# A macaron decoder step in fp32 on one core: four PSUM banks for the down projections, and a new instruction order with weight splits on ScalarE and VectorE at both feed-forward entries

## The chip, the cores and the metric

One core of one Trainium2 chip runs the whole step. The metric is device time in microseconds of that core: 2587.69 us, the median of three runs (2587.02 to 2591.2). The engines are TensorE (PE in the profile, PEld for its weight loads), VectorE (DVE), ScalarE (ACT), GpSimd (POOL) and SyncE (SP), which here issues nearly all DMAs.

## The reference, cut to what matters

The model is one layer of a decoder trunk on 1024 prompt tokens and 8 sample tokens, 1032 in all, with width 1024 and hidden width 2816:

```python
def swiglu(x, w_gate, w_up, w_down):
    return (jax.nn.silu(x @ w_gate) * (x @ w_up)) @ w_down

def decoder_layer(x, pos, lp, attend):
    h = x + 0.5 * swiglu(rmsnorm(x, lp['norm_ffn1']), lp['ffn1_w_gate'], lp['ffn1_w_up'], lp['ffn1_w_down'])
    u = rmsnorm(h, lp['norm_mix'])
    ...
    h = h + merge_branches(o_mla.astype(h.dtype), o_dil.astype(h.dtype), gates,
                           lp['w_o_mla'], lp['w_o_dil'], lp['w_out'])
    h = h + 0.5 * swiglu(rmsnorm(h, lp['norm_ffn2']), lp['ffn2_w_gate'], lp['ffn2_w_up'], lp['ffn2_w_down'])
    return h, state
```

Everything is float32. The change touches the two `swiglu` lines only.

## The kernel before, in words

**Layout.** Activations are kept transposed: `x` is 128 partitions by 8 chunks (KD) of the width by 1032 tokens. The tokens form three tiles (TILES): 352, 352 and 328. The hidden width is 22 chunks of 128 (NF), taken as 11 pairs (NPAIR).

**Products.** Each float32 product is three passes of TensorE: both operands are split into an upper part, rounded to fp32r, and a lower part, the rest, and `mm3` (lines 803 to 805) multiplies hi by hi, lo by hi and hi by lo. The results gather in `ps`, eight PSUM banks of 512 floats.

**Weights.** They come as a stream of units of 128 x 1024 (512 KB). SP loads unit n into `raw` slot n % 2 once unit n - 2 is split (`split_done`). A split writes `w_hi` and then `w_lo` into slot n % 4. GpSimd does most of them (`split_unit`, lines 706 and 709, called by `split_units` and `split_straight`); ScalarE (`split_upper`, line 1459) and VectorE (`split_lower`, line 1858) do units 0 to 3 of the first feed-forward and two units of the projection. TensorE returns slots by `unit_used`. In the loops a feed-forward is a sequence of 66 units: two gates, two ups, and the downs of the pair before.

**Entry of a feed-forward.** The norm of the input isn't known when its first weights are there. So the first pair's gate and up run on the raw input (`first_gate_up`, line 837), in the order FIRST = (0,0), (1,0), (0,1), (0,2), (1,1), (1,2), each a chunk and a tile, each with a gate and an up group of 24 matmuls. `norm` (line 808 on, matmul at 818) sums the squares of a tile over the partitions. ScalarE takes the root (`root`, line 1474), VectorE the reciprocal (line 1854). VectorE then multiplies the gate by `rstd` (line 1923), ScalarE takes the silu (1531), VectorE the product (1931) and once more `rstd` (1934), ScalarE the upper part `h_hi` (1535), VectorE the lower `h_lo` (1937). Beside this the input itself is normalised for the later pairs, chunk by chunk: `xn` on VectorE (1877), `u_hi` on ScalarE (1482), `u_lo` on VectorE (416). From the second pair on `gate_up` (line 821) uses these, its first call waiting for each chunk in its gate groups (`normed`). All of this is written out by hand: every engine runs its own list in order, and semaphores tie them. The two lists are `first_hidden` of ScalarE (line 1524 on) and of VectorE (line 1912 on).

**Steady state.** For each later pair TensorE does two calls of `gate_up` (banks 0 to 2 gate, 3 to 5 up, one a tile), then `down` of the pair before: 24 blocks of six matmuls (8 output chunks by 3 tiles), which take turns in banks 6 and 7. There are ten such `down` in each feed-forward, 20 in all, and then `last_down`. VectorE adds each block to `x` (line 1959). The hidden part of the pair is made by `hidden` of both engines (ScalarE 1547 and 1551, VectorE 1950 and 1954). Block 0's addition stands between the last product of `hidden` and its last `h_lo` (the argument `between`). `down_evac` counts additions and starts at 2.

Of the kernel before, what the change touches and what calls it, by code (L numbers as in the profile page):

```python
# [29 lines left out]
P = 128  # L30
# [36 lines left out]
RING = 4  # L67
# [34 lines left out]
def build(nc, io):  # L102
    with ExitStack() as ctx:
# [320 lines left out]

        def ss_bank(q, t):
            return t if q == 3 else 6 + t % 2 if q != 1 else 4 + t
# [272 lines left out]
        def _(pool):  # L699
# [48 lines left out]
            split_units(RING, U_PROJ + 2)  # L748
# [43 lines left out]
            split_units(U_FFN2 + RING, N_UNIT)  # L792
# [5 lines left out]
        def _(pe):  # L798
# [38 lines left out]
            def first_gate_up(q, n, released):  # L837

                for i, (c, t) in enumerate(FIRST):
                    for j in range(2):  # L840
# [16 lines left out]
                        if j == 0 and i in (0, 2, 4):  # L857
                            norm(q, i // 2)

            def down_block(p, par, s, j, m, t):  # L860
                pe.wait_ge(down_evac, 24 * p + (j + 1))
                for c in range(2):
                    a, b = mm3(ps[:, 6 + j % 2, 0:TILES[t][1]], w_hi[:, s + c, m * P:(m + 1) * P],
# [6 lines left out]
            def down(p, par, n, s):  # L870

                pe.wait_ge(split_done, n + 2)
                pe.wait_ge(h_ready, 6 * p + 6)
                for m in range(KD):
                    for t in range(NT):
                        down_block(p, par, s, NT * m + t, m, t)

            def last_down(p, n, q):
# [3 lines left out]
                for t in range(NT):  # L882
                    for m in range(KD):
                        down_block(p, 0, 0, KD * t + m, m, t)
# [3 lines left out]
            def ffn(w, n0, released):  # L888
                f0, p0 = w * NF, w * NPAIR
                first_gate_up(2 * w, n0, released)  # L890
                for i in range((NPAIR - 1) // 2):
                    for half in range(2):
# [3 lines left out]
                        gate_up(4 * i + (f0 + 2 + 2 * half), 0, n, s, 2, normed=2 * w if i + half == 0 else None)  # L896
# [547 lines left out]
        def _(act):  # L1444
# [32 lines left out]
            def upper(q, t):  # L1477
                act.wait_ge(up_ready, 3 * NF * (q // 2) + FIRST.index((1, t)) + 1)
                for m in range(KD):
# [44 lines left out]
            def first_hidden(q):  # L1524

                for i, (c, t) in enumerate(FIRST):
                    w = TILES[t][1]
                    if c == 0 and t > 0:
                        root(q, t)
                    act.wait_ge(r_applied, R_BASE[q] + 2 * i + 1)  # L1530
                    A(silu[:, i % 2, 0:w], silu[:, i % 2, 0:w], ACT.Silu).then_inc(silu_done, 1)
                    act.wait_ge(h_mul, 3 * NF * (q // 2) + i + 1)
                    if i == 0 and q > 0:
                        act.wait_ge(down_ready, 24 * NPAIR - 23)
                    A(h_hi[:, 0, c, tile(t)], h32[:, i % 2, 0:w], ACT.Copy).then_inc(h_hi_done, 1)
                    if c == 1:
                        upper(q, t)
# [311 lines left out]
        def _(dve):  # L1849
# [62 lines left out]
            def first_hidden(q):  # L1912

                f0 = 3 * NF * (q // 2)
                for i, (c, t) in enumerate(FIRST):
                    w = TILES[t][1]
                    if c == 0:
                        reciprocal(q, t)
                        dve.wait_ge(r_done, 3 * q + t + 1)
# [5 lines left out]
                    if i == 0:  # L1925
                        raw_lower(q, 2)
                    dve.wait_ge(up_ready, f0 + i + 1)
                    dve.wait_ge(silu_done, f0 + i + 1)
                    if f0 + i > 1:
# [5 lines left out]
                                    ).then_inc(h_mul, 1)  # L1935
                    dve.wait_ge(h_hi_done, f0 + i + 1)
                    V.tensor_tensor(h_lo[:, 0, c, tile(t)], h32[:, i % 2, 0:w], h_hi[:, 0, c, tile(t)].bitcast(F32),
                                    ALU.subtract).then_inc(h_ready, 1)
                    if c == 1:
                        normed(q, t)  # L1940

            def hidden(f, c, par, between=None):
                for t in range(NT):
# [7 lines left out]
                    if t == NT - 1 and between is not None:  # L1951
                        between()
# [4 lines left out]
            def add_down_block(p, j, m, t):  # L1957
                dve.wait_ge(down_ready, 24 * p + (j + 2))
                V.scalar_tensor_tensor(x[:, m, tile(t)], ps[:, 6 + j % 2, 0:TILES[t][1]], 0.5, x[:, m, tile(t)],  # L1959
                                       ALU.mult, ALU.add).then_inc(down_evac, 1)  # L1960
# [672 lines left out]
```

## Time and profile before

| | |
|---|---|
| time, median of three runs | 2587.69 us (2587.02 to 2591.2) |
| span of the profiled execution, first to last instruction | 2584.7 us |
| TensorE busy | 2481.7 us, 96% |
| VectorE, ScalarE, GpSimd busy | 1113.6, 575.7, 881.2 us (43, 22, 34%) |
| mean granted clock of TensorE | 0.985 |
| matmuls | 16119, those of `u` and `h` in the feed-forwards and the projection by 0.32 us each |
| DMA | 229 MB, mean 89 GB/s; a weight unit lands 3.2 us behind its issue |

The profiled execution's own time isn't listed apart from the three runs, so it lies 2.3 to 6.5 us above its span, and the median 3.0 above it. Busy shares overlap: a matmul's row lasts 0.32 us, but the next one starts 0.16 us after it. A time is the start from the span's beginning. The first feed-forward runs from 12 to about 790 us, attention and merge from there to 1800, the second feed-forward to 2567, and the last norm closes the span. PEclk is the granted clock as a share of 2.4 GHz.

### The profile page before, as it was taken

How to read it: one execution, taken by the hardware profiler on the slowest of the kernel's cores; microseconds unless marked ns; L12 is line 12 of the kernel's file. 1: busy time of each engine (PE TensorE's matmuls, PEld its weight loads, DVE VectorE, ACT ScalarE, POOL GpSimd, SP SyncE). 2: the span in 40 equal slices, each digit the busy share in tenths (PEclk: the TensorE clock that was granted, in tenths of full speed). 3: DMA queues.
4: the chain of work that ended last, by engine and by line, in shares of the span. 5: the costliest groups of instructions: out<-in, count | busy, mean ns of one | idle time of the engine just before them, and what ended most of it. 6: DMA issues, size and time to landing. Idle time of an engine off the chain costs nothing. (4 is left out here: it accounts for less than half of the span.)

```text
span 2584.7 us, 40647 instructions
## 1 busy us (share of the span) xinstructions
PE 2481.7 (96%) x16119; PEld 2355.6 (91%) x16119; DVE 1113.6 (43%) x1936; ACT 575.7 (22%) x1328; POOL 881.2 (34%) x451
## 2 busy tenths in 40 slices
PE   6999999999999999999999888899999999999996
PEld 6899999999999998999765567899899999999996
DVE  7523232323236864311566456655833223222226
ACT  6300000000014441211555335113400000000002
POOL 2334443334445542433000111344244333344333
PEclk9999999999999999999999899899999999999998
DMA  5122212122223332421211354552111211111111
GB/s 183 56 72 89 78 65 89 69 95 72 78 82 129 135 113 100 149 94 73 73 45 43 97 210 160 176 173 73 66 68 69 91 41 49 49 50 49 41 41 66
DMA packets 85311, 229.45 MB, mean 89 GB/s; under 512 B 8889, under 2 KB 47330, under 8 KB 84034
## 3 DMA queue, kind: packets, MB, share of 16 engines
q1 hardware_dynamic: 79066, 207.90, 23.2%
q10 hardware_dynamic: 6088, 19.23, 1.9%
q8 instruction: 127, 2.08, 0.3%
q14 instruction: 30, 0.25, 0.0%
HBM read 196.69 MB, written 74.39 MB: 105 GB/s over the span
## 5 line engine op out<-in xcount | busy, mean ns | idle before, releaser
L803 PE MATMUL ps<-u_hi,w_hi 128*128 128x352 f32 (+1 forms) x2880 | 930.3, 323 | 30.5 <-DVE w_lo L1858 12.4
L804 PE MATMUL ps<-u_lo,w_hi 128*128 128x352 f32 (+1 forms) x2880 | 922.2, 320 | 0.0
L805 PE MATMUL ps<-u_hi,w_lo 128*128 128x352 f32 (+1 forms) x2880 | 920.4, 320 | 0.0
L706 POOL TENSOR_TENSOR w_hi<-raw,zero 128x1024 fp32r<-128x1024 f32 x178 | 340.2, 1911 | 1295.3 <-PE ps L803 1119.7
L803 PEld LDWEIGHTS ps<-u_hi,w_hi 128*128 128x128 f32 x2880 | 543.5, 189 | 39.2 <-DVE w_lo L1858 12.7
L804 PEld LDWEIGHTS ps<-u_lo,w_hi 128*128 128x128 f32 x2880 | 544.0, 189 | 0.9
L805 PEld LDWEIGHTS ps<-u_hi,w_lo 128*128 128x128 f32 x2880 | 543.0, 189 | 0.0
L709 POOL TENSOR_TENSOR w_lo<-raw,w_hi 128x1024 fp32r<-128x1024 f32 x178 | 437.1, 2456 | 13.9
L1959 DVE SCALAR_TENSOR_TENSOR x<-ps,x 128x352 f32<-128x352 f32 (+1 forms) x528 | 271.0, 515 | 211.9 <-PE ps L805 211.8
L1950 DVE TENSOR_TENSOR h<-ps,silu 128x352 f32<-128x352 f32 (+1 forms) x120 | 62.0, 516 | 679.4 <-PE ps L805 679.1
L803 PE MATMUL ps<-h_hi,w_hi 128*128 128x352 f32 (+1 forms) x1056 | 341.4, 323 | 4.7 <-DVE x L1959 2.2
L804 PE MATMUL ps<-h_lo,w_hi 128*128 128x352 f32 (+1 forms) x1056 | 338.0, 320 | 0.0
L805 PE MATMUL ps<-h_hi,w_lo 128*128 128x352 f32 (+1 forms) x1056 | 337.7, 320 | 0.0
L1547 ACT ACTIVATE silu<-ps 128x352 f32<-128x352 f32 (+1 forms) x120 | 55.0, 459 | 725.1 <-PE ps L805 725.1
L803 PEld LDWEIGHTS ps<-h_hi,w_hi 128*128 128x128 f32 x1056 | 198.4, 188 | 13.4 <-DVE x L1959 12.9
L804 PEld LDWEIGHTS ps<-h_lo,w_hi 128*128 128x128 f32 x1056 | 198.8, 188 | 0.2
L805 PEld LDWEIGHTS ps<-h_hi,w_lo 128*128 128x128 f32 x1056 | 198.7, 188 | 0.0
L1551 ACT ACTIVATE h_hi<-h 128x352 fp32r<-128x352 f32 (+1 forms) x120 | 59.1, 492 | 449.4 <-DVE h L1950 449.4
L1954 DVE TENSOR_TENSOR h_lo<-h,h_hi 128x352 fp32r<-128x352 f32 (+1 forms) x120 | 91.7, 764 | 58.1 <-ACT h_hi L1551 58.1
L2099 DVE TENSOR_TENSOR stage<-ps,rstd 128x352 f32<-128x352 f32 (+1 forms) x48 | 24.5, 515 | 142.1 <-PE ps L805 138.4
L1592 ACT ACTIVATE swapped<-ps 32x352 f32<-32x352 f32 (+1 forms) x144 | 64.7, 449 | 79.9 <-PE ps L805 61.6
L1072 PE MATMUL ps<-kT,qT 128*128 128x512 f32 (+3 forms) x192 | 74.3, 497 | 2.5 <-ACT probs L1700 2.4
(289 smaller groups left out, 2669.3 us busy)
## 6 DMA issues: line engine op xcount, KB each, us to landing
raw<-in_wstream SPq DMA_DIRECT2D x186, 512.0 KB, 3.2
out_win_out<-in_cache_win SPq DMA_DIRECT2D x23, 1424.0 KB
latn<-in_cache_mla SPq DMA_DIRECT2D x128, 80.0 KB, 1.8
scratch_gates<-stage ACTq DMA_DIRECT2D x16, 516.0 KB, 2.6
out_win_out<-in_cache_win SPq DMA_DIRECT2D x7, 1168.0 KB
kv_d<-in_cache_win SPq DMA_DIRECT2D x24, 256.0 KB, 7.4
sgt<-scratch_gates SPq DMA_DIRECT2D x16, 352.0 KB, 3.6
scratch_x_mid<-x SPq DMA_DIRECT2D x1, 4128.0 KB, 22.4
```

Of the source, the lines that this page charges most:

```text
L706: nc.gpsimd.tensor_tensor(hi, raw[:, s % RAW], zero[:].to_broadcast([P, UW]), ALU.add).then_inc(w_hi_done, 1)
L709: nc.gpsimd.tensor_tensor(lo, raw[:, s % RAW], hi.bitcast(F32), ALU.subtract).then_inc(split_done, 1)
L803: a = mm(out, wh, xh, start=start, stop=False)
L804: mm(out, wh, xl, start=False, stop=False)
L805: return a, mm(out, wl, xh, start=False, stop=stop)
L1072: last = mm(ps[:, bank, 0:w], qT[i % 2][h][:, n * P:(n + 1) * P], kT[i % 2][h][:, a * P:a * P + w], start=True, stop=not diag)
L1547: A(silu[:, b, 0:w], ps[:, t, 0:w], ACT.Silu).then_inc(silu_done, 1)
L1551: A(h_hi[:, par, c, tile(t)], h32[:, b, 0:w], ACT.Copy).then_inc(h_hi_done, 1)
L1592: last = A(swapped[a:a + 32, e % 2, 0:w], ps[b:b + 32, bank, 0:w], ACT.Copy)
L1950: V.tensor_tensor(h32[:, b, 0:w], ps[:, 3 + t, 0:w], silu[:, b, 0:w], ALU.mult).then_inc(h_mul, 1)
L1954: V.tensor_tensor(h_lo[:, par, c, tile(t)], h32[:, b, 0:w], h_hi[:, par, c, tile(t)].bitcast(F32), ALU.subtract).then_inc(h_ready, 1)
L1959: V.scalar_tensor_tensor(x[:, m, tile(t)], ps[:, 6 + j % 2, 0:TILES[t][1]], 0.5, x[:, m, tile(t)], ALU.mult, ALU.add).then_inc(down_evac, 1)
```

## The change

**Down projections.** The 24 blocks of `down` go round banks 0, 3, 6 and 7 in place of 6 and 7. A block waits for the addition four blocks back; the first two, in banks 0 and 3, wait for the silu and the product of tile 0 of the pair's second chunk, which read those banks. The next pair's first gate and up group wait for the additions of blocks 20 and 21. `between` is gone: VectorE adds block 0 with the others. `last_down` keeps banks 6 and 7.

**Entries.** Units 4 to 7 of each feed-forward's stream are split by ScalarE (upper) and VectorE (lower), so GpSimd begins with unit 8. The third sum of squares goes from behind the gate of (1,1) to behind that of (0,2). Both `first_hidden` are written anew, so that the work of (0,0) to (1,2) on the one side and the pieces of the normalised input and the splits on the other are interleaved.

```diff
+        DOWN_BANK = [0, 3, 6, 7]
...
-            split_units(RING, U_PROJ + 2)
+            split_units(2 * RING, U_PROJ + 2)
...
-            split_units(U_FFN2 + RING, N_UNIT)
+            split_units(U_FFN2 + 2 * RING, N_UNIT)
...
-            def gate_up(f, c, n, s, released, normed=None):
+            def gate_up(f, c, n, s, released, normed=None, after=None):
...
                         pe.wait_ge(silu_done if j == 0 else h_mul, 3 * f + (t - 2))
+                        if after is not None and t == 0:
+
+                            pe.wait_ge(down_evac, 24 * after + (23 + j))
...
-                        if j == 0 and i in (0, 2, 4):
-                            norm(q, i // 2)
+                        if j == 0 and i in (0, 2, 3):
+                            norm(q, (i + 1) // 2)
...
                 for m in range(KD):
                     for t in range(NT):
-                        down_block(p, par, s, NT * m + t, m, t)
+                        j = NT * m + t
+                        if j < 2:
+
+                            pe.wait_ge(silu_done if j == 0 else h_mul, 3 * (2 * p + 3) + 1)
+                        else:
+                            pe.wait_ge(down_evac, 24 * p + (j - 1))
+                        down_block(p, par, s, j, m, t, DOWN_BANK[j % 4])
```

ScalarE's new list, with `gated_silu(i)` for line 1531, `hidden_upper(i)` for 1535, `upper(q, t, part)` for the `u_hi` of some chunks:

```diff
+                unit = U_FFN2 * (q // 2)
...
+                for i in range(2):
+                    gated_silu(i)
+                    hidden_upper(i)
+                root(q, 1)
+                upper(q, 0, range(0, 2))
+                root(q, 2)
+                upper(q, 0, range(2, 3))
+                gated_silu(2)
+                upper(q, 0, range(3, 4))
+                hidden_upper(2)
+                split_upper(unit + RING)
+                upper(q, 0, range(4, 6))
+                split_upper(unit + RING + 1)
+                upper(q, 0, range(6, KD))
+                gated_silu(3)
+                hidden_upper(3)
+                gated_silu(4)
+                hidden_upper(4)
+                upper(q, 1)
+                gated_silu(5)
+                hidden_upper(5)
+                split_upper(unit + RING + 2)
+                split_upper(unit + RING + 3)
+                upper(q, 2)
```

VectorE's, with `scaled` for line 1923, `product` for 1931 and 1934, `hidden_lower` for 1937, and `next_normed(t, m)` for one `xn` and the `u_lo` of the chunk before:

```diff
+                reciprocal(q, 0)
+                scaled(0)
+                raw_lower(q, 2)
+                product(0)
+                scaled(1)
+                hidden_lower(0)
+                product(1)
+                normalize(q, 0, 0)
+                hidden_lower(1)
+                next_normed(0, 1)
+                reciprocal(q, 1)
+                scaled(2)
+                next_normed(0, 2)
+                product(2)
+                next_normed(0, 3)
+                hidden_lower(2)
+                split_lower(unit + RING)
+                next_normed(0, 4)
+                next_normed(0, 5)
+                split_lower(unit + RING + 1)
+                next_normed(0, 6)
+                reciprocal(q, 2)
+                next_normed(0, 7)
+                scaled(3)
+                lower(dve, V, q, 0, KD - 1)
+                product(3)
+                hidden_lower(3)
+                scaled(4)
+                normalize(q, 1, 0)
+                product(4)
+                next_normed(1, 1)
+                hidden_lower(4)
+                for m in range(2, KD):
+                    next_normed(1, m)
+                lower(dve, V, q, 1, KD - 1)
+                scaled(5)
+                product(5)
+                hidden_lower(5)
+                split_lower(unit + RING + 2)
+                split_lower(unit + RING + 3)
+                normed(q, 2)
...
             def add_down(p):
-                for j in range(1, NT * KD):
-                    add_down_block(p, j, j // NT, j % NT)
+                for j in range(NT * KD):
+                    add_down_block(p, j, j // NT, j % NT, DOWN_BANK[j % 4])
...
                         hidden(4 * i + (f0 + 2 + 2 * half), 0, 1 - half)
-                        hidden(4 * i + (f0 + 3 + 2 * half), 1, 1 - half, lambda: add_down_block(p, 0, 0, 0))
+                        hidden(4 * i + (f0 + 3 + 2 * half), 1, 1 - half)
                         add_down(p)
```

## Rows read from the trace of the kernel before

**Rows 1.** The waits of PE: engine, line, releaser: us in total, times, longest

```profile
PE ps L803 <- DVE u_lo L416: 6.8, 15, 2.8
...
PE ps L803 <- DVE x L1959: 2.2, 6, 1.2
```

**Rows 2.** Timeline, first down projection: start, us, engine, line, operation [idle before, releaser]

```profile
126.40 0.50 DVE L1950 TENSOR_TENSOR h<-ps,silu 128x328 f32<-128x328 f32 x1 [5.61 <-PE ps L805]
...
126.60 1.90 POOL L706 TENSOR_TENSOR w_hi<-raw,zero 128x1024 fp32r<-128x1024 f32 x1 [13.80 <-PE ps L803]
...
126.93 0.48 ACT L1551 ACTIVATE h_hi<-h 128x328 fp32r<-128x328 f32 x1 [3.70 <-DVE h L1950]
...
127.36 0.53 DVE L1959 SCALAR_TENSOR_TENSOR x<-ps,x 128x352 f32<-128x352 f32 x1 [0.47 <-PE ps L805]
...
127.80 1.05 DVE L1954 TENSOR_TENSOR h_lo<-h,h_hi 128x328 fp32r<-128x328 f32 x1
...
128.58 2.53 POOL L709 TENSOR_TENSOR w_lo<-raw,w_hi 128x1024 fp32r<-128x1024 f32 x1
...
128.78 0.95 DVE L1959 SCALAR_TENSOR_TENSOR x<-ps,x 128x352 f32<-128x352 f32 x2
128.88 0.31 PE L805 MATMUL ps<-h_hi,w_lo 128*128 128x328 f32 x1
...
129.34 0.43 PE L803 MATMUL ps<-h_hi,w_hi 128*128 128x352 f32 x1
```

**Rows 3.** Timeline, the same place of the twentieth down projection, TensorE

```profile
2518.01 0.43 PE L803 MATMUL ps<-h_hi,w_hi 128*128 128x352 f32 x1 [0.20 <-DVE x L1959]
```

**Rows 4.** Windows: us, PE, PEld, DVE, ACT, POOL busy (count), PEclk, DMA share, GB/s

```profile
54.15:68.43 14.28, 5.15 (x26) 4.99 (x26) 10.24 (x16) 9.38 (x13) 0.00 (x0) 0.76 0.33 121
63.40:66.20 2.80, 2.76 (x10) 2.76 (x11) 1.57 (x3) 1.59 (x2) 0.00 (x0) 0.50 0.00 0
79.73:89.40 9.67, 6.60 (x26) 4.99 (x25) 9.31 (x16) 4.03 (x9) 1.97 (x1) 0.82 0.18 57
91.77:99.35 7.58, 6.51 (x32) 4.50 (x30) 7.31 (x17) 4.11 (x9) 0.00 (x0) 1.00 0.00 0
93.26:99.97 6.71, 5.64 (x27) 3.71 (x26) 6.48 (x15) 3.27 (x8) 0.00 (x0) 1.00 0.00 0
1827.91:1831.52 3.61, 3.61 (x27) 3.61 (x26) 3.48 (x4) 3.13 (x5) 3.14 (x2) 1.00 0.02 5
1854.69:1862.64 7.95, 5.93 (x25) 4.85 (x25) 7.58 (x12) 2.69 (x6) 2.10 (x1) 0.79 0.42 143
1866.50:1873.20 6.70, 5.62 (x26) 3.71 (x26) 6.33 (x15) 3.25 (x8) 0.00 (x0) 1.00 0.00 1
```

**Rows 5.** Timeline of the first entry, engine by engine, merged where alike

```profile
38.08 0.53 DVE L1931 TENSOR_TENSOR h<-ps,silu 128x352 f32<-128x352 f32 x1 [1.01 <-ACT silu L1531]
...
44.65 2.56 POOL L709 TENSOR_TENSOR w_lo<-raw,w_hi 128x1024 fp32r<-128x1024 f32 x1
...
44.88 4.86 DVE L1877 SCALAR_TENSOR_TENSOR xn<-x,gains,rstd 128x352 f32<-128x352 f32 x2
...
58.06 1.28 ACT L1474 ACT_TABLE_LOAD   x1
59.36 0.55 ACT L1474 ACTIVATE rstd<-ps,eps 128x352 f32<-128x352 f32 x1
...
59.94 2.35 DVE L1854 RECIPROCAL rstd<-rstd 128x352 f32<-128x352 f32 x1 [1.34 <-ACT rstd L1474]
...
62.89 0.50 ACT L1531 ACTIVATE silu<-silu 128x352 f32<-128x352 f32 x1 [1.68 <-DVE silu L1923]
```

**Rows 6.** Timeline of the start: two splits of ScalarE and VectorE

```profile
9.74 1.99 ACT L1459 ACTIVATE w_hi<-raw 128x1024 fp32r<-128x1024 f32 x2
10.81 2.36 DVE L1858 TENSOR_TENSOR w_lo<-raw,w_hi 128x1024 fp32r<-128x1024 f32 x2 [0.31 <-ACT w_hi L1459]
```

More of the change, by code:

```diff
@@ L895, in ffn @@
                         n = 12 * i + (n0 + 4 + 6 * half)
-                        gate_up(4 * i + (f0 + 2 + 2 * half), 0, n, s, 2, normed=2 * w if i + half == 0 else None)
+                        gate_up(4 * i + (f0 + 2 + 2 * half), 0, n, s, 2, normed=2 * w if i + half == 0 else None,
+                                after=2 * i + (p0 + half - 1) if i + half > 0 else None)
                         gate_up(4 * i + (f0 + 3 + 2 * half), 1, n + 2, (s + 2) % 4, 2)
@@ L1475, in root, with upper @@
                   scale=1.0 / D).then_inc(std_done, 1)
-            def upper(q, t):
-                act.wait_ge(up_ready, 3 * NF * (q // 2) + FIRST.index((1, t)) + 1)
-                for m in range(KD):
+            def upper(q, t, part=range(KD)):
+                if part[0] == 0:
+                    act.wait_ge(up_ready, 3 * NF * (q // 2) + FIRST.index((1, t)) + 1)
+                for m in part:
                     e = KD * t + m
@@ L1524, in first_hidden, with gated_silu, hidden_upper @@
             def first_hidden(q):
[L1526 to L1529, printed above, removed]
+                unit = U_FFN2 * (q // 2)
+                def gated_silu(i):
+                    w = TILES[FIRST[i][1]][1]
                     act.wait_ge(r_applied, R_BASE[q] + 2 * i + 1)
                     A(silu[:, i % 2, 0:w], silu[:, i % 2, 0:w], ACT.Silu).then_inc(silu_done, 1)
+                def hidden_upper(i):
+                    c, t = FIRST[i]
                     act.wait_ge(h_mul, 3 * NF * (q // 2) + i + 1)
@@ L1534, in first_hidden @@
                         act.wait_ge(down_ready, 24 * NPAIR - 23)
-                    A(h_hi[:, 0, c, tile(t)], h32[:, i % 2, 0:w], ACT.Copy).then_inc(h_hi_done, 1)
-                    if c == 1:
-                        upper(q, t)
+                    A(h_hi[:, 0, c, tile(t)], h32[:, i % 2, 0:TILES[t][1]], ACT.Copy).then_inc(h_hi_done, 1)
+                for i in range(2):
[22 more added lines that the diff above has]
+                upper(q, 2)
             def hidden(f, c, par, p):
@@ L1914, in first_hidden, with scaled @@
                 f0 = 3 * NF * (q // 2)
-                for i, (c, t) in enumerate(FIRST):
+                unit = U_FFN2 * (q // 2)
+                def scaled(i):
+                    c, t = FIRST[i]
                     w = TILES[t][1]
-                    if c == 0:
-                        reciprocal(q, t)
-                        dve.wait_ge(r_done, 3 * q + t + 1)
+                    dve.wait_ge(r_done, 3 * q + t + 1)
                     dve.wait_ge(gate_ready, f0 + i + 1)
@@ L1924, in first_hidden, with product @@
                                     ).then_inc(r_applied, 1)
-                    if i == 0:
-                        raw_lower(q, 2)
+                def product(i):
+                    c, t = FIRST[i]
+                    w = TILES[t][1]
                     dve.wait_ge(up_ready, f0 + i + 1)
@@ L1935, in first_hidden, with hidden_lower, next_normed, hidden @@
                                     ).then_inc(h_mul, 1)
+                def hidden_lower(i):
+                    c, t = FIRST[i]
                     dve.wait_ge(h_hi_done, f0 + i + 1)
[L1937 to L1942, printed above, removed]
+                    V.tensor_tensor(h_lo[:, 0, c, tile(t)], h32[:, i % 2, 0:TILES[t][1]],
+                                    h_hi[:, 0, c, tile(t)].bitcast(F32), ALU.subtract).then_inc(h_ready, 1)
+                def next_normed(t, m):
+                    normalize(q, t, m)
+                    if m > 0:
+                        lower(dve, V, q, t, m - 1)
+                reciprocal(q, 0)
[39 more added lines that the diff above has]
+                normed(q, 2)
+            def hidden(f, c, par):
                 for t in range(NT):
```

19 lines of the change are left out of this document (9 added, 10 removed).

## The prediction, made before the changed kernel ran

> **What bounds the kernel now.** I began with TensorE's waits. Of the names of the feed-forwards two recur there: the pieces of `u_lo`, 6.8 us in 15 waits, and the additions into `x`, 2.2 us in 6 [rows 1]. These sums are too small, because a matmul's end is modelled and covers the first part of a stop, so I went on by start times. Every matmul of a feed-forward runs at 0.16 us start to start, so whatever TensorE stands still adds to the end, and what VectorE or ScalarE save elsewhere adds nothing.
>
> The first place is the down projection [rows 2]. Block 1 of a pair's 24 blocks is read out only after VectorE has made the last piece of `h_lo`: the product starts at 126.40, ScalarE's rounding at 126.93, block 0's addition is fitted in at 127.36, `h_lo` starts at 127.80 and is held until GpSimd's operation ends (1.05 us instead of some 0.52), and the additions of blocks 1 and 2 follow at 128.78. With two banks block 3 waits for block 1: TensorE's last matmul of block 2 starts at 128.88 and the next one at 129.34, 0.46 instead of 0.15, and that one takes 0.43 where 0.32 is usual. So a pair loses 0.31 + 0.11, some 0.41 us. The first of the 20 is shown; in the twentieth the stop is the same [rows 3].
>
> The second place is the entry of each feed-forward [rows 4]. A group of matmuls of the 352-wide tiles wants 3.86 us (24 by 0.161) and of the 328-wide 3.61, which the undisturbed group at 1827.91 shows. At the first entry the gate of (1,2), the last of FIRST, took 14.28, the normed gate of tile 1 9.67, that of tile 2 6.71: losses of 10.7, 5.8 and 3.1, in all 19.6 us. At the second entry the two normed gates took 7.95 and 6.70: 4.1 + 3.1 = 7.2 us. Behind them stand two causes. GpSimd splits units 4 to 7 here, and VectorE's operations on SBUF last as long as GpSimd's: two `xn` took 4.86 us beside a 2.56 us operation [rows 5], where eight `xn` with their eight `u_lo` took 7.58 with GpSimd idle, 0.95 a pair (the stretch 91.77:99.35) [rows 4]. And ScalarE's order puts the eight `u_hi` of tile 0, a Sqrt table load (58.06), a reciprocal (2.35) and the load of Silu ahead of the silu for which the gate waits, which comes at 62.89 [rows 5].
>
> **The change: down projections.** Four banks (0, 3, 6, 7) take turns, and block 0's addition no longer comes between. `h_lo` could start at 127.46 (0.53 after the rounding's start); it is still held until GpSimd ends at 128.5, so it ends at about 128.85, and blocks 0 and 1 are added from 128.78 and 129.25 [rows 2]. Block 4 is the first that waits for an addition, block 0's, done at 129.30. Its turn on TensorE comes at 129.99 (129.03 plus six matmuls). Slack 0.65. From there an addition takes 0.47 against 0.96 for a block, so VectorE catches up. What is queued behind the later additions is only other additions. The gate and up of the next pair now wait for blocks 20 and 21; block 20 is read out while 21 to 23 are computed. The first two blocks wait for silu and product of tile 0, some 15 us old. The added waits of TensorE (two a pair) I cost at nothing, since groups with two waits run at full rate; the bounds are 0 and 20 by 0.1. Sum: 20 by 0.41 = **8.1 us**, ends 6 and 8.3.
>
> The Trainium skill (TensorE: Matmul & The Clock Gate, "A second HAM failure mode: psum-queue depth-cycling") speaks against this part: cycling through PSUM banks made one kernel's clock swing. This trace, with two banks, can't show it for four; what it would do here is rival 3.
>
> **The first entry.** Up to the product of (0,0) at 38.08 the order is the old one [rows 5]. From there I walked the new order with the rows' own distances: 0.44 to 0.5 from one VectorE operation to the next, 0.56 where the second reads the first, 0.55 to 0.6 over to ScalarE and back, 2.35 and 2.20 for a reciprocal, 1.28 for a table load [rows 5], 1.0 for a split's upper half on ScalarE and 1.15 to 1.2 for its lower on VectorE [rows 6], all without GpSimd, which now splits nothing between weight units 3 and 8. It gives:
> - product of (1,0) at 40.3, `xn` 0 and 1 and `h_lo` by 42.9; Sqrt loaded to 43.2, root of tile 1, two `u_hi`, root of tile 2 by 45.1;
> - reciprocal of tile 1 44.6 to 47.0, scaling 47.0, third `xn` 47.5, its `u_hi` 48.1, Silu loaded 48.6 to 49.9, silu of (0,1) at 49.9, product 50.5 (was 63.5). The gate of (1,2) needs that silu at 54.15, so it no longer waits: 10.7 us gone, with the low clock in it.
> - `xn`/`u_lo` 3 to 5 with weight unit 4 (lower half 54.0) and unit 5 (58.2 to 59.4), then reciprocal 60.2 to 62.4, scaling of (0,2) at 63.4, silu 63.9 to 64.4. TensorE reaches the first normed gate at 61.4 (54.15 + 3.61 + 3.61) and waits for this silu: a new stall of 3.0 us.
> - tile 1: first `xn` 67.0, last `u_lo` done 77.0. TensorE, at 64.4 + some 1.3 for a low clock + 2 by 3.86, needs the first at 73.5: no stall.
> - silu, product of (1,2) and `h_lo` to 80.1, lower halves of units 6 and 7 80.6 to 82.9, then the eight pairs of tile 2, 7.58 us for eight as from 91.77 to 99.35 [rows 4], to 90.5. The gate ends 0.62 behind the last, at 91.1, against 99.97. TensorE, there at 81.4, stands or is paced for 6.1 us.
>
> Gain **8.9 us**. The bound at the end is VectorE's queue alone, so the 3.0 us stall and its clock cost nothing more. The low clock is in the rows: over 63.40:66.20, behind the long stop, it was 0.50 (1.2 GHz) and ten matmuls filled 2.8 us, 1.3 us more than ten at 0.16 do [rows 4]; in the new order that falls in time that tile 2's wait would take anyway.
>
> **The second entry.** The chain is the same, but the root of tile 2 waits for its sum of squares, a matmul moved behind the gate of (0,2), which ends just before 1828.2 [rows 4]; ScalarE and then VectorE stand 4 to 5 us. Root 1828.8, `u_hi` 1829.2, table to 1831.0, product of (0,1) 1831.6: 1781.1 behind the first entry. Here TensorE reaches the normed gate at 1847.1, 1.6 behind the silu, so that stall is absent. Tile 1's pieces end at 1858.1, which TensorE wants from 1854.9 to 1858.3: at most 0.2 lost. Tile 2's end at 1871.6 and the gate at 1872.3, against 1873.20. Gain **0.9 us**: 4.1 saved at tile 1, and nearly all given back at tile 2, since the two halves of four splits (4.7 us on VectorE) take the place of the waits for GpSimd.
>
> A table switch on ScalarE costs 1.28 us in the row, with the Sqrt 0.02 behind its end (58.06 and 59.36) [rows 5]. The Trainium skill (ScalarE: Activation LUTs, "What ACT_TABLE_LOAD costs") puts a drain of about 1.4 us behind each. By that rule two more such terms would stand in each chain and the sum would be smaller by 4 by 1.4 = 5.6 us; the trace disagrees, as the next activation follows at once.
>
> **What hides the rest.** Unit 6 loads once unit 4 is split (55 instead of 47) and is wanted at 79.5; unit 8 loads once unit 6 is (82) and GpSimd wants it at about 95. SP's queue has only these in it. Its window copy stands behind unit 7's load and slips to about 60; nobody waits for it. GpSimd's units 8 and 9 are released by the second gate as before and take 2 by 4.5 us (as at 126.60 and 128.58) [rows 2], with 4 by 3.86 + 2 by 3.61 = 22.7 us before the down needs them. Without that cover each would cost its whole lateness. What GpSimd is spared at each entry lies beside TensorE and brings nothing directly.
>
> **Sum.** 8.1 + 8.9 + 0.9 = 17.9 us off a span of 2584.7. The median of the three runs is 3.0 above the span and I keep that distance: 2587.7 - 17.9 = **2569.8 us**. Bounds: each entry's walk has some 50 handoffs that the old order doesn't show; at 0.05 either way, 2.5 us an entry, up or down.
>
> **Rivals.**
> 1. The entries bring much less. VectorE is the bound at both; if the wait for ScalarE between half splits is longer, or other operations are held, each microsecond counts fully. For: two of its queues have no slack. Against: GpSimd is idle in this stretch. With the whole gain of the entries lost but 2 us: 2577.6.
> 2. The bank ring brings nothing, the wait going from block 3 to block 4. That takes `h_lo` held 0.65 us longer in each pair. Against: the same operation ends at GpSimd's boundary whether it starts at 127.46 or 127.80. Entries alone: 2577.9. That the ring isn't what it says I exclude: all readers' and writers' waits change together.
> 3. The ring of banks lets TensorE's clock fall in the down projections. Place: each of 20 downs. Price: 1.3 us for a low stretch as at 63.40, so 20 by 1.3 = 26 against 17.9 gained: 2569.8 + 26 = 2595.8. It decides from 14 downs with such a stretch (18.2). Against: the clock is 1.00 in the rows where TensorE is paced for 6.7 us in small waits (from 93.26 and 1866.50) [rows 4], and the ring removes a wait.
>
> **Numbers.** A measurement of this kernel can tell about 0.2%, 5.2 us. Forecast 0.77, rival 1 0.11, rival 2 0.05, rival 3 0.03, other losses within 0.2% 0.04. The bounds of the forecast reach from 2565.5 (entries better by 2 each) to about 2575; the milder half of rival 1 takes the upper end to 2576.5, and 0.17 to 0.18 stays outside. Faster: 0.77 + 0.11 + 0.05 = 0.93; same 0.04; slower 0.03.
>
> **What would show it.** Right: no `x` entry in TensorE's waits, 24 down blocks of 0.91 to 0.97; the gate of (1,2) in 3.6 us; a stall of 3 us near 61 in the first entry and none in the second; the gates of tile 2 ending near 91.1 and 1859.3 (1872.3 less 8.9 and less ten downs by 0.41); VectorE's `xn` at about 0.57 each in both. Wrong: downs that stop at block 4, `xn` of 2 us and more, or a second entry that ends over 2 us from its place.

## The result, and the profile after

The changed kernel takes 2565.51 us (median of 4 runs, 2564.88 to 2567.56) against 2587.44 in the same comparison: faster by 21.9 us. The ratio of the timed runs is 0.9912, with a 95% interval of 0.9897 to 0.9926 (the plain quotient of the two medians is 0.9915). The forecast was 2569.8, a ratio of 0.9931, with a range that ended at 2565.5, 0.9914. Direction and mechanism held; the gain was 4 us larger than forecast, and the ratio lies just beyond the range's end, by less than its own uncertainty.

The page of the changed kernel, its span and its busy row:

```profile
span 2563.5 us, 40664 instructions
...
PE 2470.6 (96%) x16119; PEld 2355.6 (92%) x16119; DVE 1106.8 (43%) x1944; ACT 577.9 (23%) x1332; POOL 845.0 (33%) x435
```

The waits of its TensorE, where [rows 1] stood, with the one on the silu:

```profile
PE ps L805 <- DVE u_lo L416: 5.5, 3, 2.7
...
PE ps L805 <- ACT silu L1545: 2.9, 1, 2.9
...
PE ps L805 <- DVE x L2048: 1.7, 3, 1.2
```

The kernel before had this line for the silu:

```profile
PE ps L803 <- ACT silu L1531: 9.1, 1, 9.1
```

The waits for `u_lo` are 3 instead of 15, and no wait for `x` is from a pair's down any more: the three that remain belong to the last down at the end. The wait for the silu was one of 9.1 us and is another one of 2.9. The first down projection, in the timeline, answers to [rows 2]:

```profile
116.87 0.50 DVE L2041 TENSOR_TENSOR h<-ps,silu 128x328 f32<-128x328 f32 x1 [5.61 <-PE ps L807]
...
117.08 1.90 POOL L708 TENSOR_TENSOR w_hi<-raw,zero 128x1024 fp32r<-128x1024 f32 x1 [13.80 <-PE ps L805]
...
117.40 0.48 ACT L1591 ACTIVATE h_hi<-h 128x328 fp32r<-128x328 f32 x1 [3.69 <-DVE h L2041]
...
117.92 1.41 DVE L2043 TENSOR_TENSOR h_lo<-h,h_hi 128x328 fp32r<-128x328 f32 x1 [0.55 <-ACT h_hi L1591]
...
119.05 2.54 POOL L711 TENSOR_TENSOR w_lo<-raw,w_hi 128x1024 fp32r<-128x1024 f32 x1
...
119.25 1.35 DVE L2048 SCALAR_TENSOR_TENSOR x<-ps,x 128x352 f32<-128x352 f32 x3
119.35 0.31 PE L807 MATMUL ps<-h_hi,w_lo 128*128 128x328 f32 x1
...
119.50 0.32 PE L805 MATMUL ps<-h_hi,w_hi 128*128 128x352 f32 x1
```

`h_lo` starts 0.52 after the rounding and is still held to GpSimd's boundary (it ends at 119.33, 0.35 behind GpSimd's operation), and three additions follow in one row. TensorE goes from block 2 to block 3 in 0.15 us and the first matmul takes 0.32: the stop is gone. Block 4's first matmul starts at 120.46, when block 0's addition (the first of the three, 0.45 each) has been done for 0.7 us.

For the rest I cut both traces at the same matmuls, the last one of a group. The windows of the changed kernel are the first entry, from the last matmul ahead of the gate of (1,2) (it belongs to the up of (1,1); some of the expectations below call it the up of (0,1)) to the end of tile 2's normed gate, the first pair's 24 blocks, the next pair's, the stretch between the feed-forwards (from the last of the 24 blocks of the tenth down of the first to the first output block), and the second entry, from the last output block to the end of tile 2's gate. The columns are those of [rows 4]:

```profile
53.75:90.28 36.53, 30.70 (x170) 28.96 (x169) 32.02 (x59) 15.66 (x30) 0.00 (x0) 0.91 0.28 98
116.53:139.09 22.56, 22.56 (x145) 22.56 (x145) 13.53 (x25) 0.48 (x1) 8.68 (x4) 1.00 0.15 48
184.37:207.10 22.73, 22.73 (x145) 22.73 (x145) 13.53 (x25) 0.48 (x1) 8.69 (x4) 1.00 0.32 111
750.49:1697.94 947.45, 895.43 (x6191) 786.88 (x6190) 504.87 (x900) 344.53 (x868) 273.09 (x149) 0.98 0.34 117
1784.66:1856.52 71.86, 69.16 (x417) 67.72 (x415) 58.98 (x99) 35.76 (x65) 4.46 (x2) 0.95 0.19 68
```

And the same five of the kernel before:

```profile
53.99:99.81 45.82, 32.54 (x170) 28.46 (x169) 37.73 (x61) 20.54 (x36) 9.12 (x4) 0.89 0.18 62
126.06:149.09 23.03, 22.88 (x146) 22.61 (x145) 13.21 (x25) 0.48 (x1) 8.67 (x4) 1.00 0.14 47
194.36:217.58 23.22, 23.09 (x147) 22.82 (x146) 13.23 (x25) 0.48 (x1) 8.67 (x4) 1.00 0.29 109
764.64:1713.12 948.48, 897.62 (x6192) 788.39 (x6190) 503.96 (x901) 344.33 (x869) 272.86 (x149) 0.97 0.34 117
1799.84:1873.04 73.20, 70.11 (x417) 66.38 (x415) 64.73 (x95) 35.04 (x63) 22.97 (x10) 0.98 0.19 69
```

The ledger of the two spans, 2584.7 less 2563.5:

| place | before | after | gain | predicted |
|---|---|---|---|---|
| start, up to the first entry | 53.99 | 53.75 | 0.24 | 0 |
| first entry | 45.82 | 36.53 | 9.3 | 8.9 |
| ten pairs, first feed-forward | 664.8 | 660.2 | 4.6 | 4.1 |
| stretch between | 948.5 | 947.5 | 1.0 | 0 |
| second entry | 73.20 | 71.86 | 1.3 | 0.9 |
| ten pairs, second feed-forward | 664.9 | 660.2 | 4.7 | 4.1 |
| sum | | | 21.2 | 17.9 |

The medians differ by 0.7 us more than the two spans: the median lies 2.7 above the profiled span before, and 2.0 after.

Inside the first entry, three windows of the changed kernel: the gate of (1,2), the stop ahead of the first normed gate, and ten matmuls behind it; then the gates of tile 2 in both entries.

```profile
53.91:57.53 3.62, 3.62 (x26) 3.62 (x26) 2.92 (x5) 1.60 (x3) 0.00 (x0) 1.00 0.33 114
60.98:64.20 3.22, 0.31 (x4) 0.07 (x2) 3.05 (x6) 0.97 (x2) 0.00 (x0) 0.99 0.69 232
64.20:67.20 3.00, 3.00 (x10) 3.00 (x11) 2.30 (x6) 0.97 (x2) 0.00 (x0) 0.50 0.46 197
81.23:90.44 9.21, 6.29 (x26) 4.93 (x26) 8.85 (x18) 4.11 (x9) 0.00 (x0) 0.81 0.37 114
1847.23:1856.68 9.45, 6.75 (x26) 6.04 (x26) 8.90 (x19) 4.24 (x10) 0.00 (x0) 0.64 0.62 215
```

The gate of (1,2) runs undisturbed in 3.62 (it was 14.28). The stop at 61 is there, 3.22 from start to start, and the clock behind it is 0.50, ten matmuls in 3.00 us. Tile 2's gates take 9.2 and 9.4 us instead of 6.7: VectorE is busy for 8.85 of 9.21.

### The profile page after: what moved, and what is told of

Read it like the earlier page. It is cut to its first block and busy times, and to the rows that moved or that the text cites. A ratio compares the mean times of both kernels' runs of the same rounds, so it can differ in the third digit from the quotient of the medians.

```text
span 2563.5 us, 40664 instructions
## 1 busy us (share of the span) xinstructions
PE 2470.6 (96%) x16119; PEld 2355.6 (92%) x16119; DVE 1106.8 (43%) x1944; ACT 577.9 (23%) x1332; POOL 845.0 (33%) x435
## 5 line engine op out<-in xcount | busy, mean ns | idle before, releaser
L708 POOL TENSOR_TENSOR w_hi<-raw,zero 128x1024 fp32r<-128x1024 f32 x170 | 324.0, 1906 | 1310.5 <-PE ps L805 1136.2
L711 POOL TENSOR_TENSOR w_lo<-raw,w_hi 128x1024 fp32r<-128x1024 f32 x170 | 416.7, 2451 | 13.3
L2043 DVE TENSOR_TENSOR h_lo<-h,h_hi 128x352 fp32r<-128x352 f32 (+1 forms) x120 | 98.9, 824 | 69.1 <-ACT h_hi L1591 69.1
L1466 ACT ACTIVATE sq<-x 128x352 f32<-128x352 f32 (+1 forms) x96 | 45.4, 489 | 139.1 <-DVE x L2048 58.9
```

The costliest lines, as they stand in the source:

```text
L708: nc.gpsimd.tensor_tensor(hi, raw[:, s % RAW], zero[:].to_broadcast([P, UW]), ALU.add).then_inc(w_hi_done, 1)
L711: nc.gpsimd.tensor_tensor(lo, raw[:, s % RAW], hi.bitcast(F32), ALU.subtract).then_inc(split_done, 1)
L1466: A(sq[:, e % 4, 0:TILES[t][1]], x[:, m, tile(t)], ACT.Square).then_inc(sq_done, 1)
L2043: V.tensor_tensor(h_lo[:, par, c, tile(t)], h32[:, b, 0:w], h_hi[:, par, c, tile(t)].bitcast(F32), ALU.subtract).then_inc(h_ready, 1)
```

## The experiments

All runs side by side, each window from one profile. The time is the median of the timed runs, and the ratio is to runs of the kernel before made beside them (median 2588.34 us for runs 1 to 4, 2588.85 for 5 to 8), so compare ratios and windows rather than times. "Pairs" is the 24 blocks of the first and of the second down.

| run | time | ratio (95%) | first entry | pairs | stretch between | second entry |
|---|---|---|---|---|---|---|
| before | 2587.44 | 1 | 45.82 | 23.03, 23.22 | 948.5 | 73.20 |
| changed | 2565.51 | 0.9912 (0.9897 to 0.9926) | 36.53 | 22.56, 22.73 | 947.5 | 71.86 |
| 1 ring alone | 2576.6 | 0.9956 (0.9940 to 0.9973) | 46.77 | 22.56, 22.73 | 946.9 | 73.20 |
| 2 entries alone | 2577.11 | 0.9956 (0.9939 to 0.9973) | 36.50 | 23.03, 23.16 | 948.9 | 71.93 |
| 3 new order, GpSimd splits | 2567.32 | 0.9921 (0.9904 to 0.9937) | 37.06 | 22.56, 22.73 | 942.9 | 75.05 |
| 4 units 6 and 7 late | 2559.97 | 0.9895 (0.9873 to 0.9917) | 33.11 | 22.57, 22.74 | 948.2 | 68.84 |
| 5 old order, new splitters | 2569.24 | 0.9923 (0.9906 to 0.9939) | 37.56 | 22.56, 22.73 | 951.6 | 72.44 |
| 6 early norm | 2562.14 | 0.9895 (0.9878 to 0.9911) | 35.96 | 22.57, 22.73 | 947.8 | 68.67 |
| 7 late and early | 2556.27 | 0.9875 (0.9859 to 0.9892) | 33.70 | 22.57, 22.74 | 943.7 | 66.02 |
| 8 three banks | 2574.15 | 0.9940 (0.9923 to 0.9956) | 36.49 | 23.00, 23.15 | 948.6 | 71.64 |
| 9 changed, again | 2565.1 | single run | 36.45 | 22.56, 22.73 | 947.0 | 71.62 |
| 10 before, again | 2590.62 | single run | 46.30 | 23.03, 23.20 | 952.4 | 73.19 |

### 1. The ring alone

The kernel before, with the changed kernel's banks and waits, and `between` removed:

```diff
-                pe.wait_ge(down_evac, 24 * p + (j + 1))
...
-    mm3(ps[:, 6 + j % 2, ...], ...)
+    mm3(ps[:, DOWN_BANK[j % 4], ...], ...)
...
-   hidden(4 * i + (f0 + 3 + 2 * half), 1, 1 - half, lambda: add_down_block(p, 0, 0, 0))
+   hidden(4 * i + (f0 + 3 + 2 * half), 1, 1 - half)
```

> The kernel before with the four-bank ring alone, entries as they were. Theory A (the ring takes away block 3's stop and the small waits of the other blocks too): a pair's 24 blocks take 22.57 and 22.73 us in turn, as in the changed kernel, instead of 23.03 and 23.2; 20 by 0.46 = 9.2 us less, ratio 0.9964. Theory B (my predicted term, block 3's stop alone): 8.1 us less, a pair 22.62 and 22.80. Theory C (part of what the changed kernel gained in its downs comes from the entries): a pair above 22.8. The entries stay at 14.3, 9.7, 6.7 and 8.0, 6.7 us.

The windows of its first two downs:

```profile
127.53:150.09 22.56, 22.56 (x145) 22.56 (x145) 13.53 (x25) 0.48 (x1) 8.67 (x4) 1.00 0.13 48
195.37:218.10 22.73, 22.73 (x145) 22.73 (x145) 13.52 (x25) 0.48 (x1) 8.69 (x4) 1.00 0.32 111
```

22.56 and 22.73: theory A. The whole gain of the downs comes from this part of the change (four banks together with block 0's addition moved; the two weren't run apart). It is 0.47 and 0.49 in the pairs shown, and 4.6 + 4.7 = 9.3 us in 20 by the ledger, where I had 8.1. TensorE is busy for the full 22.56.

### 2. The entries alone

The changed kernel with the downs as before (the diff of run 1 turned round).

> The changed kernel with the old downs (two banks, block 0's addition between). If the two parts add up: first entry as in the changed kernel (normed gate of tile 2 ends near 90.3), second entry 1.3 us shorter than before, downs 23.03 and 23.2 us; 9.5 + 1.3 = 10.8 us less, ratio 0.9958. If the 1.05 us that the stretch between the feed-forwards lost comes from the change it is here or in the run with the ring alone; if it is scatter of that stretch, it differs from run to run by about as much.

Its entries and downs:

```profile
54.01:90.51 36.50, 31.32 (x170) 29.01 (x169) 32.01 (x59) 15.61 (x30) 0.00 (x0) 0.91 0.28 98
116.76:139.79 23.03, 22.88 (x146) 22.61 (x145) 13.21 (x25) 0.48 (x1) 8.67 (x4) 1.00 0.14 47
1790.95:1862.88 71.93, 69.24 (x416) 67.81 (x415) 58.99 (x99) 35.73 (x66) 4.46 (x2) 0.95 0.19 68
```

Both entries are those of the changed kernel to 0.1 us, the downs those of before. So the parts add up: the ratios of runs 1 and 2 multiply to 0.9912, and the windows show nothing given back or shared.

### 3. The new order with GpSimd's splits

```diff
-            split_units(2 * RING, U_PROJ + 2)
+            split_units(RING, U_PROJ + 2)
...
-            split_units(U_FFN2 + 2 * RING, N_UNIT)
+            split_units(U_FFN2 + RING, N_UNIT)
...
-                split_upper(unit + RING)
...
-                split_lower(unit + RING)
```

and so for the other three units.

> The changed kernel, but units 4 to 7 of each feed-forward are split by GpSimd again. Theory A (who splits matters: VectorE is held by GpSimd): VectorE's operations are held by 4 splits, some 10 us an entry, and spared 4.7 us of lower halves, so each entry ends 4 to 6 us later than in the changed kernel (normed gate of tile 2 near 95 to 96), ratio to before 0.9945 to 0.996. Theory B (the order alone makes the gain): it ends at 90.3 or, with the lower halves gone from VectorE, as early as 86.

Its two entries:

```profile
54.32:91.38 37.06, 31.27 (x171) 27.23 (x170) 34.16 (x58) 13.76 (x29) 9.32 (x4) 0.95 0.21 79
1781.23:1856.28 75.05, 70.76 (x417) 66.31 (x416) 65.36 (x95) 32.00 (x61) 22.68 (x10) 0.98 0.19 68
```

The first entry takes 37.06, only 0.5 more than with the splits moved: theory A fell there, and the order alone makes nearly the whole gain. At the second it is 3.2 more than the changed kernel's, and 1.8 more than before: there the order alone loses. Part of the new order there is the wait for tile 2's root: ScalarE's root comes after 6.08 us idle at 1810.05, and VectorE stands 4.98 us ahead of the product of (0,1) in this run too. Run 6 prices that wait in the changed kernel; how much of the 1.8 is its share wasn't tried. VectorE's timeline at the first entry shows which of its operations GpSimd holds:

```profile
44.06 1.78 DVE L416 TENSOR_TENSOR u_lo<-xn,u_hi 128x352 fp32r<-128x352 f32 x1 [1.23 <-ACT u_hi L1496]
45.76 2.34 DVE L1890 RECIPROCAL rstd<-rstd 128x352 f32<-128x352 f32 x1
...
48.58 1.75 DVE L1913 SCALAR_TENSOR_TENSOR xn<-x,gains,rstd 128x352 f32<-128x352 f32 x1
50.25 2.72 DVE L416 TENSOR_TENSOR u_lo<-xn,u_hi 128x352 fp32r<-128x352 f32 x1
```

GpSimd's operations there:

```profile
43.56 1.89 POOL L708 TENSOR_TENSOR w_hi<-raw,zero 128x1024 fp32r<-128x1024 f32 x1 [3.72 <-PE ps L805]
45.53 2.55 POOL L711 TENSOR_TENSOR w_lo<-raw,w_hi 128x1024 fp32r<-128x1024 f32 x1
48.05 1.89 POOL L708 TENSOR_TENSOR w_hi<-raw,zero 128x1024 fp32r<-128x1024 f32 x1
50.02 2.57 POOL L711 TENSOR_TENSOR w_lo<-raw,w_hi 128x1024 fp32r<-128x1024 f32 x1
```

`u_lo` and `xn`, which read two large operands from SBUF, end 0.4 behind one of them. The reciprocal, with one SBUF operand, takes 2.34 beside GpSimd's second, as it does alone (2.35 in [rows 5]). The new order puts a reciprocal and the wait for the silu into this stretch, so little is left to be held; the silu of (0,1) comes at 52.17 and the gate of (1,2) again needs no wait.

### 4. Units 6 and 7 late

```diff
+                upper(q, 2)
                 split_upper(unit + RING + 2)
                 split_upper(unit + RING + 3)
-                upper(q, 2)
...
+                normed(q, 2)
                 split_lower(unit + RING + 2)
                 split_lower(unit + RING + 3)
-                normed(q, 2)
```

> The changed kernel with the halves of units 6 and 7 moved behind tile 2's normalised pieces on both engines. Theory A (VectorE's queue alone sets when tile 2's gate ends): the gate ends earlier by the halves and their wait, 2.3 to 2.7 us an entry, and units 6 and 7 are ready at about 89.5, before TensorE wants them at 91.2; 4.6 to 5.4 us less than the changed kernel, ratio to before 0.9896. Theory B (the units come too late then): the gain comes back as a stop before the second gate, time as the changed kernel's.

```profile
54.19:87.30 33.11, 29.35 (x170) 26.11 (x169) 28.64 (x57) 14.36 (x29) 0.00 (x0) 1.00 0.21 76
1782.46:1851.30 68.84, 67.90 (x416) 65.38 (x415) 56.11 (x97) 34.43 (x64) 4.46 (x2) 1.00 0.11 41
```

3.4 and 3.0 us less than in the changed kernel, and TensorE doesn't stop for units 6 and 7: theory A, by somewhat more than the halves themselves (2.7). The clock is 1.00 in both windows, against 0.91 and 0.95 in the changed kernel; what part of the gain is the clock's wasn't separated. That the order of these queues sets the end of tile 2's gate is shown by this run. That it is VectorE's and not ScalarE's rests on their busy time over that gate, 8.85 and 4.11 us of 9.21, since both engines' halves were moved. The timed runs scatter more than in the others (2556.57 to 2567.86), so the 5.5 us against the changed kernel is less sure than the 6.4 of the windows.

### 5. The old order with the new splitters

Run 1's kernel, with the splits put behind tile 0's and tile 1's pieces, on both engines:

```diff
                     if c == 1:
                         upper(q, t)
+                        if t < 2:
+                            for n in (2 * t, 2 * t + 1):
+                                split_upper(U_FFN2 * (q // 2) + RING + n)
```

> The kernel with the ring alone, plus the splits of units 4 to 7 on ScalarE and VectorE, put behind tile 0's and tile 1's normalised pieces in the old order; the third corner beside the ring alone (old order, GpSimd splits) and the new order with GpSimd's splits. From the up of (0,1) (its last matmul) to the end of tile 2's normed gate the corners so far took 46.8 us (old order, GpSimd), 37.1 (new order, GpSimd) and 36.5 (both). Theory A (order and splits take away the same wait, either one does at the first entry): 38 to 40. Theory B (the splits alone do little, since ScalarE's silu still stands behind tile 0's pieces): 43 or more. At the second entry, where the new order with GpSimd's splits was 1.8 us slower than before: the splits alone should gain 2 to 4 us by either theory.

```profile
54.51:92.07 37.56, 31.00 (x170) 28.89 (x169) 30.24 (x53) 18.35 (x32) 0.00 (x0) 0.91 0.26 93
1790.62:1863.06 72.44, 69.21 (x416) 66.46 (x415) 59.47 (x99) 38.97 (x67) 4.45 (x2) 0.98 0.20 70
```

37.56, a little under theory A's band: at the first entry either half of the change does the work. The four corners there are 46.8 (old order, GpSimd; 45.8 and 46.3 in the two profiles of the kernel before), 37.1 (new order), 37.6 (new splitters) and 36.5 (both), so 9.7 and 9.2 alone and 10.2 together, each less by up to 1 when taken from the kernel before. They don't do it in the same way. In the window of the kernel before VectorE is busy for 37.7 us and idle for 8.1; the new order alone leaves 34.2 and 2.9, the new splitters alone 30.2 and 7.3, and here TensorE still stops for 3.66 us ahead of the gate of (1,2). At the second they are 73.2, 75.0, 72.4 and 71.9: the new order costs 1.8 with GpSimd and gains 0.6 without it. The expected 2 to 4 us there was too much, it was 0.8.

### 6. The early norm

```diff
-                        if j == 0 and i in (0, 2, 3):
-                            norm(q, (i + 1) // 2)
+                        if j == 0 and i in (0, 2):
+                            norm(q, i // 2)
+                        if j == 0 and i == (3 if q == 0 else 2):
+                            norm(q, 2)
```

> The changed kernel, but the third sum of squares of the second entry stands behind the second one, one gate earlier, where its squares are long added. Theory A (ScalarE's root of tile 2, and VectorE behind it, wait for that matmul): VectorE's idle 4.95 us ahead of the product of (0,1) shrinks to about 2, as at the first entry, and the second entry ends about 3 us earlier; the first is unchanged; ratio to before 0.990. Theory B (the wait is hidden elsewhere): entry 2 as in the changed kernel, 71.9 us from the last output block to the end of tile 2's normed gate.

The row of VectorE's timeline ahead of which it stood idle at the second entry, in the changed kernel:

```profile
1816.30 0.52 DVE L1974 TENSOR_TENSOR h<-ps,silu 128x352 f32<-128x352 f32 x1 [4.95 <-issue]
```

The same row here:

```profile
1814.42 0.53 DVE L1976 TENSOR_TENSOR h<-ps,silu 128x352 f32<-128x352 f32 x1 [1.99 <-issue]
```

And the window of the second entry here:

```profile
1785.77:1854.44 68.67, 67.79 (x416) 65.41 (x415) 58.91 (x99) 35.67 (x65) 4.45 (x2) 1.00 0.20 70
```

The idle time went from 4.95 to 1.99 us and the entry from 71.86 to 68.67: theory A, 3.2 us. The first entry was to stay as it was and took 35.96 here, 0.6 less, but it also began 1.3 us later (55.07 against 53.75), in a stretch that this edit doesn't touch.

### 7. Late and early together

> Units 6 and 7 late and the early norm together. If both act on VectorE's one queue they add until tile 2's gate is no longer paced: second entry 71.9 - 3.0 - 2.8 = 66 us, first entry as with the late units alone (33.1 from the up of (0,1)); 2.8 us less than the run with the late units, ratio to before 0.9885. If something else paces the gate, the second entry stays at 68.8.

```profile
54.29:87.99 33.70, 29.36 (x171) 26.13 (x169) 29.23 (x57) 14.36 (x29) 0.00 (x0) 1.00 0.21 75
1778.58:1844.60 66.02, 66.02 (x416) 65.42 (x415) 56.28 (x97) 34.59 (x64) 4.46 (x2) 1.00 0.12 43
```

In the second entry TensorE is now busy for all of the 66.02 us and its clock is 1.00: nothing is left there. The kernel takes 2556.27 us, 0.9875 (0.9859 to 0.9892), the lowest of all. Against run 4 the two entries together are 2.2 us shorter; the rest of the 3.7 us between the times isn't theirs, and the stretch between was 4.5 us shorter by scatter in the profile. The first entry keeps its stop at 61 and the paced gates of tiles 1 and 2, 7.4 us in 33.7.

### 8. Three banks

```diff
-        DOWN_BANK = [0, 3, 6, 7]
+        DOWN_BANK = [0, 6, 7]
...
-                            pe.wait_ge(down_evac, 24 * p + (j - 1))
+                            pe.wait_ge(down_evac, 24 * p + j)
```

with `j % 3` for `j % 4` and the waits of the first block and of the next pair's gate to match.

> The changed kernel with its downs in three banks (0, 6, 7). My own reckoning of the ring (block 0's addition done at 119.8, block 3's turn at 119.5): a stop of 0.3 and a slower first matmul at block 3 remains, but the small waits of the other blocks go: a pair 22.9 to 23.0 and 23.1 us, 7 us more than the changed kernel in 20 downs. If three banks do as well as four: 22.6 and 22.7, no difference.

```profile
116.61:139.61 23.00, 22.85 (x147) 22.58 (x146) 13.53 (x25) 0.48 (x1) 8.67 (x4) 1.00 0.13 47
184.88:208.03 23.15, 23.02 (x146) 22.75 (x145) 13.52 (x25) 0.48 (x1) 8.67 (x4) 1.00 0.30 109
```

The stop at block 3:

```profile
119.34 1.35 DVE L2047 SCALAR_TENSOR_TENSOR x<-ps,x 128x352 f32<-128x352 f32 x3
119.44 0.31 PE L807 MATMUL ps<-h_hi,w_lo 128*128 128x328 f32 x1
119.90 0.43 PE L805 MATMUL ps<-h_hi,w_hi 128*128 128x352 f32 x1 [0.15 <-DVE x L2047]
```

23.00 and 23.15: my reckoning of when additions are done holds, and three banks in this order keep the whole stop at block 3. From the start of block 2's last matmul to that of block 3's it is 1.37 us, as in the kernel before; in the changed one it is 0.95. Here block 3 waits for block 0's addition, which is the first behind `h_lo`, just where block 1's stood in the kernel before. Only 0.03 and 0.07 of the gain in the first two downs come with three banks. So with block 0's addition behind `h_lo`, it takes the fourth bank to remove the stop.

Three banks with block 0's addition left between the product and `h_lo` weren't run. By [rows 2] block 4 would then be the first to wait for an addition behind `h_lo`, block 1's, done at about 129.3 by my estimate, and its turn comes at 129.99: that kernel might have removed the stop as well.

### 9 and 10. Both kernels once more

> The changed kernel as it is, profiled once more, to see what the stretch between the feed-forwards (from the last down block of the first to the first output block) does by itself. In eight profiles so far it took 942.9 to 951.6 us, 948.5 before and 947.5 in the changed kernel. If the 1.0 us it lost is scatter, this one differs from 947.5 by some tenths to some us, while the first entry from its up of (0,1) stays at 36.5, the downs at 22.57 and 22.73 and the second entry at 71.9. If it belongs to the change: 947.5 again, to 0.2.

> The kernel before, profiled once more for the same reason. Scatter: the stretch between the feed-forwards differs from 948.5 by up to some us, the downs stay at 23.03 and 23.2. The first entry, whose holds by GpSimd depend on where the operations fall, may differ by a microsecond (45.8 here, 46.8 in the run with the ring alone). Otherwise: 948.5 and 45.8 again, to 0.2.

The stretch between the feed-forwards in the two:

```profile
750.62:1697.63 947.01, 895.77 (x6192) 786.66 (x6191) 504.68 (x901) 343.78 (x869) 272.95 (x149) 0.98 0.34 117
```

```profile
764.89:1717.25 952.36, 906.35 (x6192) 797.43 (x6190) 504.98 (x901) 344.36 (x869) 272.58 (x149) 0.96 0.34 117
```

The same kernel gave 948.5 and 952.4 before, 947.5 and 947.0 changed. In all twelve profiles it lies between 942.9 and 952.4, with no tie to the edits, which don't touch it. So the 1.0 us of the ledger is within scatter. The two longest, 952.4 here and 951.6 in run 5, have the lowest granted clocks over it (0.96 and 0.97) and the longest busy time of TensorE (906 and 902 us, against 893 to 898 in the others); that explains a part at most, and the rest wasn't tried. The start, up to the first entry, isn't touched either and ends between 53.75 and 55.07, so its 0.24 us in the ledger is scatter too. The downs and the second entry repeat to 0.25 us, the first entry of the kernel before to 1 us.

## Why the prediction was right or wrong

**The down projections**: the mechanism held (runs 1 and 2), the term was mis-sized: 8.1 for 9.3 us. The step that failed is "So a pair loses 0.31 + 0.11, some 0.41 us". The stop itself was nearly right: from the start of block 2's last matmul to that of block 3's it is 1.37 us before and 0.95 after, 0.42. But the other blocks of the pair, which I had taken as undisturbed, hold another 0.05 to 0.07 us of small waits. The sum then lost a little more: 20 by 0.41 is 8.2, and 20 by 0.42 is 8.4, so neither the 8.1 nor the upper end of 8.3 follows from it. I should have compared the whole 24 blocks with six matmuls each at the gates' rate. That makes 22.66 us by the prediction's own 3.86 and 3.61 a group, against 23.03 and 23.22 in the first two downs of the kernel before: 0.46 on average.

**Slack at block 4**: 0.65 predicted, about 0.7 shown; the later `h_lo` is held as I said. Rival 1 is out by run 2, rival 2 by run 1, rival 3 by the granted clock of 1.00 in the windows of the downs. The clock swings that the Trainium skill describes (TensorE: Matmul & The Clock Gate, "A second HAM failure mode: psum-queue depth-cycling") aren't seen with these four banks.

**The first entry**: 8.9 for 9.3. The walk held step by step: the third scaling was laid at 47.0 and stands at 46.81, the silu of (0,1) at 49.9 and 49.67, unit 4's lower half at 54.0 and 53.74, the stop of 3.0 us at 61.4 is one of 3.2 at 61.0 (from start to start, 3.1 without the matmul's own time), the gate's end of 91.1 is 90.4; about 0.24 of each is the earlier start. What I got wrong is the weight of the causes. I wrote of two causes and took both remedies as needed; runs 3 and 5 show that either remedy alone takes 9 of the 10 us. Both relieve VectorE's queue, one its idle and one its busy time; that this is why they don't add is my reading. The sum was nearly right because I walked the queue and didn't add remedies.

**The second entry**: 0.9 for 1.3. TensorE needed no stop at the first normed gate, tile 1 ran at full rate, and tile 2 gave most back, as said. VectorE's idle time behind the root of tile 2, 4 to 5 us predicted, is 4.95; run 6, which takes away 3.0 of it, gains 3.2. The gate of tile 2 was to end near 1859.3 and ends at 1856.7. This is more than 2 us from its place, one of the signs of being wrong that I had named: 1.0 of the 2.6 us comes from the stretch between, 0.5 from the downs, 0.4 from each entry and 0.2 from the start.

**The table loads**: 1.28 with the next activation right behind, in the changed kernel too (48.37 and 49.67), so the drain of 1.4 us that the Trainium skill names (ScalarE: Activation LUTs, "What ACT_TABLE_LOAD costs") doesn't appear behind the load. Nor does it ahead of it: the load at 41.71 starts 0.02 behind the end of the rounding before it (41.19 and 0.50). With it the first entry would have ended at about 93, an estimate from 90.3 and two drains.

**The range**: with the ring at 9.3 the forecast would have been 2568.6. The rest all fell on the same side: 0.8 us in the entries, 0.2 at the start and 1.0 in the stretch between (both scatter), and 1.0 in the distance from span to median. I had kept that at 3.0 from one profile of the kernel before; it is 2.0 in the changed kernel, and every later run lies 1.8 to 2.2 above its own span. The lower end was also drawn too tight by my own bounds: 2.5 us an entry and the ring's 0.2 give 2564.6, not 2565.5. And I gave nothing for a stretch of 950 us of many small waits, whose scatter alone is wider than that; the lower end should have been near 2562. That the time fell just at the old end, and not well inside or outside, is chance.

## What to carry to other kernels

Size a repeated stop by the whole repeated stretch against its ideal length, not by the one interval in which it shows: the small waits beside it go with the same cure. Where one engine's queue bounds a stage, walk that queue in the new order with the durations of the old one, and look first at what stands in it that nobody wants soon; here moving two splits at each entry behind the pieces that TensorE waits for took 6.4 us off the windows, and a sum of squares one gate earlier 3.2 (8.7 together, run 7). And give the range the scatter of the stretches that the change doesn't touch.

## What the runs showed of the hardware that was not expected

GpSimd doesn't hold every VectorE operation on SBUF. Those with two large SBUF operands ended 0.3 to 0.4 us behind a GpSimd operation (in run 3, 1.75 to 2.72 us for 0.5). A reciprocal with one ran in its usual 2.34 beside GpSimd's operation from 45.53 to 48.08 (run 3). Operations with one operand in PSUM (the additions at 119.25, 0.45 each) weren't held either. That the number of SBUF operands decides, and not the kind of operation, fits these rows but wasn't tested by itself.

After the 3.22 us stop TensorE's granted clock was 0.50 (1.2 GHz) for 3 us; in run 4 the stop at the same place was 2.62 us from start to start, and the clock was 1.00 over the stop and the gates behind it. In run 7 a stop of 3.19 us there left it at 1.00 too, while in run 6 one of 2.66 us was followed by 0.74 over the next 2.9 us. So the length alone doesn't tell which it will be, and that wasn't followed up. Around the stops at tile 2 of the changed kernel (2.97 and 3.02 us from start to start) it was down as well, 0.81 and 0.64 over the gates. The rows give no sign that this cost much: VectorE was busy for 8.85 and 8.90 us of these gates' 9.21 and 9.45.
